# First attention of a two-layer model with keys on the partitions and 512 queries at a time, instead of 128 queries on the partitions

## The reference, cut to what matters

```
s = jnp.einsum('bqhgd,bkhd->bhgqk', qblk, k, preferred_element_type=jnp.float32) * scale
p = jax.nn.softmax(s, axis=-1).astype(v.dtype)
return jnp.einsum('bhgqk,bkhd->bqhgd', p, v)
```

## Time and profile before

| what | us |
|---|---|
| median of 3 runs (lowest, highest) | 4312.03 (4309.52, 4312.44) |
| the profiled execution, its own time | 4309.44 |
| its span, first to last instruction | 4307.4 |
| attention stage in it: first pool product to first projection product | 360.02 to 672.04 |
| one unit in the steady part | 6.19 |
| PE busy in 400 to 500 us | 92.4 of 100 |
| DVE busy in 400 to 500 us | 63.0 of 100 |

### The profile page before, as it was taken

How to read it: one execution, slowest core, us unless ns; L and a number is a source line. 1 busy time by engine, 2 the same in 40 slices (tenths; PEclk the granted TensorE clock), 3 DMA queues, 4 the chain that set the end, 5 groups by cost and what they waited for, 6 DMA issues and landing times.

```text
span 4307.4 us, 51362 instructions
## 1 busy us (share of the span) xinstructions
PE 4077.1 (95%) x20059; PEld 3120.8 (72%) x20059; DVE 2023.9 (47%) x2420; ACT 1270.5 (29%) x1883; POOL 1333.3 (31%) x791
## 2 busy tenths in 40 slices
PE   7999998899999998889999999999999899999998
PEld 5776775457777774578888788876766678878886
DVE  4263662864676776571443233324444654323322
ACT  3122330212222221231332232224554633223222
POOL 0530000011111111022344444434444544444443
PEclk8999999999999999999999999999999999999999
DMA  6111004331121115651233333321000033333333
GB/s 229 39 39 59 0 0 141 142 136 65 68 76 68 68 53 191 155 163 49 83 93 97 98 97 97 98 89 69 25 25 25 16 113 94 96 99 97 97 98 107
DMA packets 118829, 372.05 MB, mean 86 GB/s; under 512 B 18004, under 2 KB 33679, under 8 KB 114896
## 3 DMA queue, kind: packets, MB, share of 16 engines
q1 hardware_dynamic: 98960, 296.38, 22.1%
q0 software_dynamic: 12784, 59.50, 3.8%
q10 hardware_dynamic: 6928, 13.96, 0.9%
HBM read 329.37 MB, written 38.06 MB: 85 GB/s over the span
## 4 chain that ended last, share of the span: by engine, by line
PE 63%; issue 16%; DVE 8%; POOL 6%; DMA 3%; ACT 2%; SPq 0%; POOLq 0%; ACTq 0%; DVEq 0%
PE banks L276 22%; PE banks L3104 6%; POOL w_parts L261 6%; PE banks L1230 5%; PE banks L291 5%; PE banks L696 5%; PE banks L1605 4%; PE banks L982 3%; PE banks L3178 2%; PE banks L3207 2%; DVE neg_max L1061 2%; DMA w_ring<-in_weights 1%; PE banks L3194 1%; PE banks L1586 1%; PE banks L1636 1%
## 5 line engine op out<-in xcount | busy, mean ns | idle before, releaser
L261 POOL TENSOR_TENSOR w_parts<-w_ring,w_parts 128x1024 fp32r<-128x1024 f32 x344 | 843.1, 2452 | 1089.3 <-ACT w_parts L254 1087.2
L276 PE MATMUL banks<-x_high,w_parts 128*128 128x512 f32 x2944 | 912.1, 390 | 0.0
L254 ACT ACTIVATE w_parts<-w_ring 128x1024 fp32r<-128x1024 f32 x344 | 364.5, 1060 | 1281.7 <-PE banks L276 1273.8
L276 PEld LDWEIGHTS banks<-x_high,w_parts 128*128 128x128 f32 x2944 | 552.6, 188 | 116.8 <-issue 2.1
L276 PE MATMUL banks<-x_low,w_parts 128*128 128x512 f32 x1472 | 572.8, 389 | 0.0
L276 PE MATMUL banks<-hidden_high,w_parts 128*128 128x512 f32 x1600 | 482.2, 392 | 6.0 <-POOL w_parts L261 6.0
L3312 DVE TENSOR_TENSOR_SCAN arena<-arena,flags 128x128 f32<-128x128 f32 (+3 forms) x192 | 248.7, 1308 | 250.3 <-ACT arena L3253 248.5
L276 PEld LDWEIGHTS banks<-hidden_high,w_parts 128*128 128x128 f32 x1600 | 301.7, 189 | 71.0 <-POOL w_parts L261 6.8
L2993 DVE TENSOR_TENSOR hidden_high<-banks,gate_temps 128x512 f32 (+1 forms) x88 | 60.9, 692 | 571.7 <-PE banks L276 571.6
L276 PEld LDWEIGHTS banks<-x_low,w_parts 128*128 128x128 f32 x1472 | 276.3, 188 | 59.0 <-issue 1.9
L1230 PE MATMUL banks<-parts_b,w_ring_low 128*128 128x512 f32 x896 | 303.6, 405 | 14.7 <-DVE resid_low L394 9.7
(11 more groups left out here) (456 smaller groups left out, 6488.4 us busy)
## 6 DMA issues: line engine op xcount, KB each, us to landing
w_ring<-in_weights SPq DMA_DIRECT2D x488, 512.0 KB, 3.5
arena<-in_hy_dft SPq DMA_DIRECT2D x11, 1536.0 KB, 6.1
s_cl<-arena POOLq DMA_DIRECT2D x4, 1152.0 KB, 6.7
resid<-in_xT ACTq DMA_DIRECT2D x2, 2048.0 KB, 26.3
resid<-in_xT POOLq DMA_DIRECT2D x1, 4096.0 KB, 14.0
arena<-in_fn_seq POOLq DMA_DIRECT2D x1, 4096.0 KB, 18.0
resid_spill<-resid POOLq DMA_DIRECT2D x1, 4096.0 KB, 12.6
s_e<-arena POOLq DMA_DIRECT2D x4, 1024.0 KB, 5.1
```

Source lines behind the costliest of these rows:

```text
L254: nc.scalar.activation(WP[:, g % 2, 0, :], WR[:, (g % RING) * TILE:(g % RING + 1) * TILE], ACT.Identity).then_inc(w_hi, 1)
L261: nc.gpsimd.tensor_tensor(WP[:, g % 2, 1, :], WR[:, (g % RING) * TILE:(g % RING + 1) * TILE], WP[:, g % 2, 0, :].bitcast(F32), ALU.subtrac ...
L276: mm = nc.tensor.matmul(PS[:, bank + h // H, :], w[a][:, k % KB, :], srcs[b][:, k, at + h:at + h + H], start=(first and i + q == 0), stop= ...
```

## The change

Queries and keys change places. The work is now 12 "halves" g (a head and 512 of its queries), each of ten blocks b of 128 keys; block i = 10g + b. For a block the keys are the stationary operand and 512 queries the moving one, so probabilities come out with the keys on the partitions and go into the values product as they are: the turns, the copies out of PSUM and the query copies fall away.

- **Parts.** ACT writes the high parts of keys (1280 columns, once for each key head) and queries (512 columns a half); POOL writes the low parts. The key parts lie in `XLOW`, over five eighths of `XT`.
- **Maxima.** For each half four products of the high parts alone with queries on partitions (`tops`, 3 F32R instructions of 512, 512 and 256 columns, into banks 4 to 6), and DVE's maximum of each (`top`, 1280 columns). They are made one half ahead. PE turns the 128x4 maxima into 4x128 (`turned`), DVE spreads them to a 4x512 tile that holds each query's maximum in one of four rows and zero in the others (`shift`).
- **Scores.** Three F32R products of parts and, in the same bank, a fourth one that subtracts the maxima: stationary `MINUS` (-1, 4 rows by 128 columns), moving `SHIFT` (4 rows by 512). Banks 0 to 3 in turn. ACT's exponential has neither bias nor sum; it writes one of six buffers `PROB`.
- **Values.** One F32 product of 512 columns a block, summed over the ten blocks in bank 7.
- **Sums.** DVE adds up a half's ten `PROB` tiles (`summed`, nine additions of 512 columns, both inputs in SBUF); one F32 product with `ONES` adds over the partitions (`denominator`), DVE takes its reciprocal in PSUM and multiplies (`divided`), after it has multiplied the values with the gate (`gated`).
- **Around it.** The reload of `XT` is cut in two: blocks 5 to 7 at the start, blocks 0 to 4 (2.6 MB), which the key parts lie over, after the last scores. EvOut's first three modulation tiles may start once `gated` of the last half is done. The stage is written out, without hardware loops.

The diff, cut to its core:

```
     class Attention(Stage):
-        done = [(a_o, UNITS), (pme, 4)]
+        done = [(a_o, 2 * HALVES), (pme, 4)]
...
         def pe(p):
...
+            def tops(g, t):
+                p.wait_ge(a_hi, parts_made(g))
+                p.wait_ge(a_top, 4 * g + t)
+                if t == 0 and g >= 3:
+                    p.wait_ge(a_o, 2 * (g - 2))
                 for c in range(0, KEYS, H):
                     w = min(H, KEYS - c)
+                    mm = nc.tensor.matmul(PS[:, 4 + c // H, 0:w], QPARTS[g % 2][0][:, t * P:(t + 1) * P],
+                                          KPARTS[0][kv_of(g)][:, c:c + w], start=True, stop=True)
+                mm.then_inc(a_mx, 1)
+            def turned(g):
+                p.wait_ge(a_top, 4 * g + 4)
+                if g:
+                    p.wait_ge(a_sh, g)
+                nc.tensor.transpose(PS[0:4, 6, 384:512], TOP[g % 2], IDENT[:, :]).then_inc(a_tt, 1)
+            def scores(i):
...
+                if i >= 4:
+                    p.wait_ge(a_p, i - 3)
+                out_ = PS[:, i % 4, :]
+                for n, (x, y) in enumerate(((0, 0), (0, 1), (1, 0))):
+                    nc.tensor.matmul(out_, KPARTS[x][kv][:, b * P:(b + 1) * P], q[y], start=(n == 0), stop=False)
+                if b == 0:
+                    p.wait_ge(a_sh, g + 1)
+                nc.tensor.matmul(out_, MINUS[0:4, :], SHIFT[g % 2][0:4, :], start=False, stop=True).then_inc(a_s, 1)
+            def values(i):
+                g, b = divmod(i, KBL)
+                p.wait_ge(a_p, i + 1)
+                if b == 0 and g:
+                    p.wait_ge(a_o, 2 * g - 1)
+                nc.tensor.matmul(PS[:, 7, :], V0[:, b, kv_of(g) * HD:(kv_of(g) + 1) * HD], PROB[i % 6],
+                                 start=(b == 0), stop=(b == KBL - 1)).then_inc(a_pv, 1)
+            def denominator(g):
+                p.wait_ge(a_ad, KBL * (g + 1))
+                p.wait_ge(a_top, 4 * min(g + 3, HALVES))
+                nc.tensor.matmul(PS[:, 4, :], ONES[:, :], ACCP[g % 2], start=True, stop=True).then_inc(a_dn, 1)
...
+            tops(0, 2)
+            tops(0, 3)
+            turned(0)
+            scores(0)
+            scores(1)
+            for n in range(BLOCKS // 2):
+                g, s = divmod(n, KBL // 2)
+                ahead = g + 1 < HALVES
+                for i in (2 * n + 2, 2 * n + 3):
+                    if i < BLOCKS:
+                        scores(i)
+                if s < 2 and ahead:
+                    tops(g + 1, 2 * s)
+                if s == 2 and ahead:
+                    turned(g + 1)
+                if s == 3 and g:
+                    denominator(g - 1)
+                values(2 * n)
+                values(2 * n + 1)
+                if s < 2 and ahead:
+                    tops(g + 1, 2 * s + 1)
+            denominator(HALVES - 1)
...
         def act(a, link):
...
+            for i in range(BLOCKS):
+                a.wait_ge(a_s, i + 1)
+                if i >= 6:
+                    a.wait_ge(a_pv, i - 5)
+                    a.wait_ge(a_ad, i - 5)
+                nc.scalar.activation(PROB[i % 6], PS[:, i % 4, :], ACT.Exp, scale=SCALE0).then_inc(a_p, 1)
+                if i % KBL == 0 and i // KBL + 1 < HALVES:
+                    queries_high(i // KBL + 1)
...
         def dve(v, link):
...
+            for n in range(BLOCKS // 2):
+                g, s = divmod(n, KBL // 2)
+                ahead = g + 1 < HALVES
+                if s == 0 and g:
+                    gated(g - 1)
+                summed(2 * n)
+                summed(2 * n + 1)
+                if s < 2 and ahead:
+                    top(g + 1, 2 * s)
+                    top(g + 1, 2 * s + 1)
+                if s == 2 and ahead:
+                    shift(g + 1)
+                if s == 3 and g:
+                    divided(g - 1)
+            gated(HALVES - 1)
+            divided(HALVES - 1)
...
         def pool(g_, link):
...
+            g_.wait_ge(a_s, BLOCKS)
+            g_.wait_ge(x_back, 16)
+            g_.dma_start(XT[:, 0:5, :], xt[:, 0:5, :]).then_inc(x_back, 16)
...
     class EvOut(Stage):
...
-            wait_done(p, Attention.done)
+            p.wait_ge(a_o, 2 * HALVES - 1)
             for n in range(8):
...
                     mod_rows(p, st, 4 * n + i, 7, i * P)
+                if n == 0:
+                    wait_done(p, Attention.done)
                 matmul_tile(p, st, 4 * n + 3, n, MT)
...
-            v.wait_ge(x_back, 16)
+            v.wait_ge(x_back, 32)
```

More of the change, by code:

```diff
@@ L921, in _build, with s0_parts, kv_of, parts_made @@
     MT = HT
[L922 to L925, removed]
-    pm, pme = sem("pool_mm"), sem("pool_out")
[L927 to L931, removed]
+    XLOW_ = XLOW[:, :, :].rearrange("p k t -> p (k t)")
+    KPARTS = [[XLOW_[:, (2 * x + kv) * KEYS:(2 * x + kv + 1) * KEYS] for kv in range(N_KV)] for x in range(2)]
+    def s0_parts(at, words):
+        return PTA_[:, A_S0 - 12800 + at:A_S0 - 12800 + at + words]
+    QPARTS = [[s0_parts((2 * i + x) * H, H) for x in range(2)] for i in range(2)]
+    SHIFT = [s0_parts(4 * H + i * H, H) for i in range(2)]
+    PROB = [ar(A_S0 + 6 * H + i * H, H) for i in range(6)]
+    ACCP = [ar(A_S0 + 6400 + i * H, H) for i in range(2)]
+    MINUS = s0_parts(7424, P)
+    TOP = [ar(A_S0 + 7552 + 4 * i, 4) for i in range(2)]
+    a_hi, a_lo, a_mx, a_top, a_tt, a_sh = (sem("a_" + x) for x in ("hi", "lo", "mx", "top", "tt", "sh"))
+    a_s, a_p, a_ad, a_pv, a_dn, a_o = (sem("a_" + x) for x in ("s", "p", "ad", "pv", "dn", "o"))
+    pm, pme = sem("pool_mm"), sem("pool_out")
+    KBL = KEYS // P
+    HALVES = 2 * N_HEADS
+    BLOCKS = KBL * HALVES
+    def kv_of(g):
+        return g // (HALVES // N_KV)
+    def parts_made(g):
+        return g + 2 if g < 2 else g + 3
     class Attention(Stage):
@@ L964, in pe, with pool_part @@
             p.wait_ge(tab_in, 96)
[L965 to L979, removed]
+            def pool_part(b, h):
+                if b:
+                    p.wait_ge(pme, h + 1)
+                nc.tensor.matmul(PS[:, 2 + h, :], POOLW_T[:, b, :], AV[:, b, 8 + h * H:8 + h * H + H],
+                                 start=True, stop=True).then_inc(pm, 1)
@@ new lines, in summed @@
+            def summed(i):
+                g, b = divmod(i, KBL)
+                acc = ACCP[g % 2]
+                v.wait_ge(a_p, i + 1)
+                if b == 1:
+                    if g >= 2:
+                        v.wait_ge(a_dn, g - 1)
+                    nc.vector.tensor_tensor(acc, PROB[(i - 1) % 6], PROB[i % 6], ALU.add).then_inc(a_ad, 2)
+                elif b > 1:
+                    v.wait_ge(a_ad, i)
+                    nc.vector.tensor_tensor(acc, acc, PROB[i % 6], ALU.add).then_inc(a_ad, 1)
@@ new lines, in dve @@
+            pool_out(0)
+            pool_out(1)
+            top(0, 0)
+            pool_out(2)
+            top(0, 1)
+            pool_out(3)
+            top(0, 2)
+            top(0, 3)
+            shift(0)
+            for n in range(BLOCKS // 2):
[12 more added lines that the diff above has]
+                    divided(g - 1)
```

185 lines of the change are left out of this document (65 added, 120 removed).

## The result

The changed kernel takes 4325.38 us (median of 9 runs, 4321.62 to 4329.09), the one before 4312.44, measured beside it (9 runs, 4308.59 to 4314.24): ratio 1.0035, interval 1.0025 to 1.0044. That is 12.9 us slower, where 7.6 was forecast; it lies in the range of 4303 to 4336, and past the 0.2% (8.6 us) that was to be "the same".

What follows compares the result with a forecast made beforehand. PE was taken to bound the attention stage. A projection starting 9.3 us later (681.3 against 672.04) and -1.7 in EvOut gave +7.6 us: 4317.0 profiled, 4319.6 for the median, range 4303 to 4336.

Steps and rivals of the forecast that it cites:

- The bound and the half: Attention loop: PE sets the pace at 25.5 us per half, against 17.7 for DVE and 6.8 for ACT.
- The switch: Each block's 4-row score product: changing rows in and out costs PE 0.39 us, 46.8 over 120 blocks.
- no switch: Rival: the 4-row product goes through like the others, 46.8 us fall out of the blocks; 4273.9 us, chance 0.14.
- dearer switch: Rival: the switch at each block's fourth product costs 0.51 us, 14.4 more in all; 4334 us, chance 0.20.
- cheaper: Rival: the switch at each block's fourth product costs 0.33 us, -7.2 in all; 4312.4 us, chance 0.04.
- The start: Stage's start: first scores at 371.7, four maxima 2.3 us apart, plus 3.0 us for half clock in the loop (bounds 0 and 5).
- The steady part: Attention loop: PE's blocks, maxima products, turns and denominators take 301.4 us in all, waits costed at nothing.
- The end: Stage's end: last denominator, reciprocal, product and hand-offs take 5.0 us from the last values product to the projection.
- step 3: Within a half: DVE waits for the denominator, then needs 4.05 us, additions queued behind; costed at nothing.
- the -1.7: EvOut, step 1: the fourth weight tile, behind fewer bytes in the DMA engines, takes 6.0 us instead of 7.72.
- forecast case: Main case, chance 0.60, own range 4311 to 4329: 0.36 of it the same, 0.24 slower.
- DVE* rival: Attention loop: DVE's additions take 2.38 us, not 0.69, and DVE becomes the bound; 89 more, 4408 us, chance 0.02.

Runs made afterwards that it cites:

- e4: Changed kernel plus 18 unused products filling PE's waits between the first maxima at the stage's start: 4320.27 us, ratio to before 1.0027.
- e3_tail: Changed kernel with the last half's denominator and division of the half before moved from its step 3 to step 1: 4322.99 us, ratio to before 1.0033.
- e6_xt_twice: Changed kernel with the 2.6 MB reload of XT after the last scores sent twice: 4326.33 us, ratio to before 1.0039.
- e1_full_rows: Changed kernel with each block's fourth score product padded with zero rows from 4 to 128 rows: 4276.04 us, ratio to before 0.9928.
- e8: Changed kernel with padded rows, busy start, earlier last division, 11 filling products before the projection, second key head's parts two halves later: 4279.41 us, ratio to before 0.9932.
- e7: Changed kernel with padded rows, busy start, earlier last division and 22 filling products before the projection: 4275.64 us, ratio to before 0.9924.

## Why the prediction was right, and where it was off

**The bound and the half: right.** PE is the bound, DVE at 67 to 70% ("about 70%"), and the half takes 25.37 us ("25.5").

**The switch: right, and shown.** Forecast 0.39, read off rows with 64 rows; measured 0.40 in the block. Taking it away brought 3.48 us a half and 45.0 in the stage, halving it brought half, and 64 rows cost what 4 do. It also settles that the whole gain which exchanging queries and keys could have given went there: without it the change is some 35 us faster than before (4276.0 against 4310.8 in the same comparison). The rival *no switch* had 4273.9 and the padded kernel measured 4276.0, but that is luck: the rival's terms make a stage of 275.6 us, the trace has 281.8, and shorter parts outside the stage made up for it. The Trainium skill, "TensorEngine Tiling (Array Packing)", Key Properties, says that a change of tiling mode drains the TensorE; these runs agree with it for a change of rows, which costs 0.40 us in and out. The *dearer switch* (0.51) and the *cheaper* one (0.33) fell: this operand costs 0.40 also between F32R products. For fewer columns the prediction used the same rule, 0.4 us for each `turned`, and that was wrong: its follower starts 0.11 behind it. The 11 in the loop had been put 3.2 us too high.

**The start: the step that was mis-sized.** Two terms. The first scores came 12.56 us after the stage's start (357.04 to 369.60), not 11.7. At full clock they come 12.0 after it (`e4`): the four maxima follow each other by 2.5 us, not 2.3, since a `tops` took some 0.85 until DVE could start, not 0.75, while the first went 0.3 earlier than forecast. The other 0.6 is the clock, which the prediction let fall only in the loop. There it took half clock for 6 us and 3.0 us for it. The windows show 0.50 up to 380 and 0.70 in 380 to 385, so until 383: 13.4 us from 369.6. What that cost is read against `e4`, whose clock stays full: from the first scores to the scores behind the second `tops` the changed kernel takes 14.2 us and `e4` 9.7, of which 1.2 are its wait, so 5.8 are lost in the loop, outside the bound of 5 that was given. It is less than half of 13.4, since a block of scores takes 2.30 us at half clock and 1.33 at full: an F32R product goes from 0.233 to 0.43 only. The prediction had taken the length of the dip from the kernel before, and no row there shows what sets it; the kernels here, with the same start, have 3.4 to 17 us of it. Keeping PE busy took all 6.4 away and brought the wait of 1.2, so 5.2 net.

**The steady part** gave back 0.6. A half's terms in the forecast add up to 25.4 us (the "25.5" is rounded up) and it measured 25.37: what `turned` had too much, the switches (0.01 each) and small gaps had too little. Together: +0.3 (the maxima), +3.4 (the clock, 6.4 for 3.0) and -0.6 make the last values end 319.4 us after the start, where 316.3 was forecast.

**The end: a wait was missed.** 7.4 us from the last values to the projection instead of 5.0. The prediction had written down that DVE's additions queue behind the division in step 3, and that in a half this costs nothing since PE has 10 us more to do; it didn't apply the same sentence to the last half, where nothing follows. `e3_tail` shows these 2.4 us.

**EvOut: wrong sign.** The fourth tile did come earlier, 6.72 instead of 7.72 (forecast 6.0), so -1.0; but the first projection tile took 15.48 instead of 13.95, at half clock until 686.8 behind the longer wait at the end, +1.5. `e6_xt_twice` shows that the working behind the -1.7, bytes ahead of a tile, was not sound. The further +2.2 lies in later tiles: the second tile and the next three waits were 1.2 shorter, and the sixth and seventh, with the wait between them, 3.4 longer, with half clock in 779 to 782 and 799 to 806. That is scatter as far as these traces go: `e1_full_rows`, whose EvOut has the same instructions, ran them at full clock, and such kernels differ by up to 6 us (145.9 to 151.9).

**The sum.** Stage +5.5 over its forecast, EvOut +4.4, against which the two parts that the change doesn't touch came out 1.2 shorter in the traces. The range held, and this trace's EvOut, among the longest of those with the same instructions, is luck on the slow side. "The same" had been called likeliest with 0.40, of the forecast case 0.36, though slower had 0.46 over all cases; by its own line of 8.6 us "the same" did not come about. The terms that lost most were the two ends of the stage, where PE stops being covered. The *DVE* rival did not come about, but its mechanism is real: an addition takes 3.02 us (`e4`) and up to 3.25 (`e8`) beside POOL, 0.69 alone. With POOL at 7% it costs nothing in the steady halves of 25.4 us, and 1.2 to 2.4 us once in a stage where PE is at full clock from the start or has shorter halves.

## What to carry to other kernels

A product with few rows among products of 128 rows isn't cheap: it costs its columns plus some 0.4 us for the change of rows in and out, where few columns among 128 cost nothing of the kind. Pad it with zero rows to 128 if its operands can be laid out so, or put the small products side by side. When a stage is costed from its steady part, look at both ends on their own: what PE waits for before its loop can also slow the loop's first products by the clock (6.4 us here), and what queues behind a long DVE instruction without cost in the middle stands in the path at the end.

## What was not expected of the hardware

- The switch costs the same at 4 and at 64 rows, and a second 4-row product behind the first adds only its own 0.23 us. A stationary operand of 4 columns and 128 rows pays no switch.
- Zero rows are free: 128 rows by 512 columns take 0.23 us, as 4 rows do beside the switch.
- DVE's additions and POOL's subtractions don't share, they take turns. An addition that began during a subtraction ended 0.54 to 0.56 us after it (the changed kernel at 375.01, `e4`, `e7`, twice in `e8`). A subtraction that came due while an addition ran took 0.5 us more (3.40 instead of 2.91 in `e8`), and beside an addition that began after it none (2.92 in `e4`).
- The same start of the stage had half clock for anything from 3.4 to 17 us, and none where filling products stood in PE's waits.
- 2.6 MB more on POOL's queue delayed a tile of SP's queue by 0.66 us only and POOL's own next transfer by 8.0.
